# Computing the u side of the 48 first keys densely, beside the v side, in a layer with a product-key expert step

## What is computed

```python
def peer_ffn(h, w_query, sub_keys, expert_u, expert_v):      # 8 heads, 128 x 128 experts of 2048 channels
    q = (h @ w_query).reshape(B, S, PEER_HEADS, 2, PEER_HALF)
    scores = jnp.einsum('bshcd,hckd->bshck', q, sub_keys)
    s_top, i_top = lax.top_k(scores, PEER_TOPK)               # 16 first keys, 16 second keys
    cand_idx = i_top[..., 0, :, None] * PEER_KEYS + i_top[..., 1, None, :]
    best, pos = lax.top_k(cand, PEER_TOPK)                    # 16 experts for each token and head
    gate = jax.nn.softmax(best, axis=-1)
    ...
    u = jnp.take(expert_u, ic, axis=0)                        # 128 rows of 8 KB for each token
    act = jax.nn.gelu(jnp.einsum('ckd,cd->ck', u, xc), approximate=False)
    vv = jnp.take(expert_v, ic, axis=0)
    return jnp.einsum('ck,ckd->cd', gc * act, vv)
```

## Time and profile before

| | us |
|---|---|
| median of 3 runs | 2037.04 (2035.09 to 2037.86) |
| the profiled execution | 2035.97 |
| its span in the trace | 2034.4 |
| end of the query matmuls, groups 0 and 1 under way | 845 |
| end of group 1 on DVE | 882.4 |
| end of group 7 / 12 / 13 / 15 on DVE | 1184.0 / 1482.2 / 1541.8 / 1645.4 |

### The profile page before, as it was taken

One profiled execution on the slowest core, in us unless ns is written; L12 is line 12 of the kernel. 1 busy time (PEld: TensorE's weight loads), 2 busy tenths in 40 slices (PEclk: granted clock), 3 DMA queues, 4 the chain that ended last, 5 costly groups with the idle time before them and its releaser, 6 DMA issues.

```text
span 2034.4 us, 18656 instructions
## 1 busy us (share of the span) xinstructions
PE 1557.4 (77%) x6346; PEld 995.1 (49%) x6347; DVE 1368.9 (67%) x2217; ACT 540.0 (27%) x919; POOL 1050.3 (52%) x647
## 2 busy tenths in 40 slices
PE   7999999999999999622222245656555899999986
PEld 6888888888888898400000011222113554444432
DVE  5463453233333348499889998788889976887977
ACT  5344453345443510110001012232214630000001
POOL 4443343444432413266556675566556737887752
PEclk9999999999999999855555555555555579999998
DMA  8986455665546689599999999999999999999997
GB/s 209 242 176 140 148 186 158 191 189 187 173 133 210 194 298 379 198 409 420 419 416 415 410 417 419 419 418 418 420 418 419 419 357 376 413 415 392 395 422 309
DMA packets 158409, 648.33 MB, mean 319 GB/s; under 512 B 26150, under 2 KB 31342, under 8 KB 96366
## 3 DMA queue, kind: packets, MB, share of 16 engines
q0 software_dynamic: 73728, 450.98, 54.2%
q1 hardware_dynamic: 83824, 195.16, 30.6%
q10 hardware_dynamic: 768, 1.05, 0.2%
HBM read 729.91 MB, written 2.10 MB: 360 GB/s over the span
## 4 chain that ended last, share of the span: by engine, by line
PE 42%; DMA 21%; DVE 15%; issue 11%; POOL 9%; ACTq 0%; ACT 0%; SPq 0%; DVEq 0%; POOLq 0%
PE acc L1673 10%; PE acc L1675 10%; PE acc L1674 10%; DMA u_ring<-in_peer_u_dram,idx 6%; PE acc L2002 4%; DMA v_low<-in_peer_v_dram,idx 4%; DMA u_mid<-in_peer_u_dram,idx 4%; DMA v_more<-in_peer_v_dram,idx 3%; DVE u_ring L1497 3%; DVE u_ring L1495 3%; DVE y_sum L1543 2%; POOL u_ring L628 2%; DMA u_high<-in_peer_u_dram,idx 2%; PE acc L1963 1%; POOL v_high L636 1%
## 5 line engine op out<-in xcount | busy, mean ns | idle before, releaser
L577 POOL TENSOR_TENSOR w_lo<-raw,w_hi 128x1024 fp32r<-128x1024 f32 x112 | 274.7, 2453 | 424.7 <-ACT w_hi L716 424.3
L1673 PE MATMUL acc<-w_hi,t_hi 128*128 128x512 f32 x896 | 355.0, 396 | 0.0
L1675 PE MATMUL acc<-w_hi,t_lo 128*128 128x512 f32 x896 | 349.5, 390 | 0.0
L1674 PE MATMUL acc<-w_lo,t_hi 128*128 128x512 f32 x896 | 349.0, 390 | 0.0
L628 POOL DMA_INDIRECT u_ring<-in_peer_u_dram,idx x160 | 211.6, 1323 | 251.3 <-DVE dots L1497 212.2
L1076 DVE TENSOR_TENSOR w_lo<-raw,w_hi 128x1024 fp32r<-128x1024 f32 x112 | 153.0, 1366 | 265.4 <-ACT w_hi L716 265.3
L716 ACT ACTIVATE w_hi<-raw 128x1024 fp32r<-128x1024 f32 x224 | 237.0, 1060 | 330.5 <-PE acc L1675 287.3
L1495 DVE CUSTOM_DVE_ANT_0 u_ring<-u_ring,hn 128x1024 f32<-128x1024 f32 x160 | 195.6, 1223 | 56.2 <-DMA u_ring<-in_peer_u_dram,idx 50.1
L2041 PE MATMUL misc<-v_low,blocks 128*32 128x512 f32 x368 | 88.5, 1060 | 177.7 <-DMA v_low<-in_peer_v_dram,rows_at 160.6
L2041 PE MATMUL misc<-v_high,blocks 128*32 128x512 f32 x368 | 85.0, 1017 | 157.7 <-DMA v_high<-in_peer_v_dram,rows_at 157.7
L1497 DVE CUSTOM_DVE_ANT_0 u_ring<-u_ring,hn 128x1024 f32<-128x1024 f32 x160 | 195.3, 1221 | 0.0
(11 more groups left out here) (302 smaller groups left out, 2313.7 us busy)
## 6 DMA issues: line engine op xcount, KB each, us to landing
u_ring<-in_peer_v_dram SPq DMA_DIRECT2D x48, 1024.0 KB, 8.8
raw<-in_w_in_dram SPq DMA_DIRECT2D x64, 512.0 KB, 6.5
raw<-in_xattn_wk_dram SPq DMA_DIRECT2D x32, 512.0 KB, 4.5
raw<-in_xattn_wv_dram SPq DMA_DIRECT2D x32, 512.0 KB, 3.9
raw<-in_w_out_dram SPq DMA_DIRECT2D x32, 512.0 KB, 4.7
...
```

The costliest lines, as they stand in the source:

```text
L577: nc.gpsimd.tensor_tensor(w_lo[:, j % RING, :, :], raw[:, j % RING, :, :], w_hi[:, j % RING, :, :].bitcast(F32), ALU.subtract).then_inc(lo ...
L1673: nc.tensor.matmul(o, xh, w_hi[:, s, kk, :], start=first, stop=False)
L1674: nc.tensor.matmul(o, xh, w_lo[:, s, kk, :], start=False, stop=False)
L1675: ins = nc.tensor.matmul(o, xl, w_hi[:, s, kk, :], start=False, stop=last)
```

## The change

For the same 48 first keys the u side is computed densely too.

- SP loads 48 whole tiles of u (128 experts of one first key, 1 MB) into two slots. PE turns a tile in 4 **steps** of 4 transposes (`turn_tile`), ACT copies each quarter out of PSUM (`copy_turned`), and PE multiplies it with the turned hidden rows of all 256 tokens (`tile_dots`, 4 matmuls with 256 columns in a step). ACT takes the gelu of the whole tile into the tables `wT0` and `wT1` (`act_tile`). The 192 steps lie between the picks of groups 2 to 12 on PE and ACT, about 17.5 in a group. The hidden rows are scaled once: DVE widens the factor, PE turns it, ACT copies it, and POOL multiplies `t2f` in 4 instructions in group 2.
- `gather_u` and all v gathers leave out the rows of the 48 keys. The v groups 14 and 15 of the high half are bounded too (`WHOLE` is gone). A u row that is not loaded leaves old data in its slot; its activation is set to zero in `weights`.
- What is scattered is the gate alone, and DVE multiplies it into the tables (`apply_acts`, which takes the place of ACT's copy L943): one instruction of 384 elements in a batch for the low half, three of 128 for the high half. The 16 low batches are all in group 13 (`UNTIL`), one for each k; the 16 high ones in the second half of group 14 and the first half of group 15.
- The half dots write to four bf16 scratch rows and not over the row, and each waits for the half dot that wrote the same scratch before it.
- Slots: u has 5 from group 2 on (was 7); low v has 2 in groups 2 to 7, 3 in groups 8 to 12, 4 after (was 4 to 7). Low v gathers begin in group 2 and are 6 in a group up to group 7, 11 in groups 8 to 12, 12 or 13 after.
- `take_experts(0)` moves from group 1 to group 2, after pick 1; `weights` of the group before moves from pick 2 to pick 9. The order of the first slots of the late stage changes.

```diff
@@ SP
+            for t in range(DENSE):
+                if t < 2:
+                    sp.wait_ge(peer_used, PC)
+                else:
+                    sp.wait_ge(uT_done, 4 * (t - 1))
+                sp.dma_start(u_tile[:, t % 2, :], u_rows[(FROM + t) * KEYS:(FROM + t + 1) * KEYS, :]).then_inc(tile_landed[t % 2], 16)
@@ POOL
                 nc.gpsimd.indirect_dma_start(
                     out=u_slot(n), out_offset=None, in_=u_rows,
-                    in_offset=bass.IndirectOffsetOnAxis(ap=idx[:, p, k:k + 1], axis=0)).then_inc(u_landed[u_index(n)], 16)
+                    in_offset=bass.IndirectOffsetOnAxis(ap=idx[:, p, k:k + 1], axis=0),
+                    bounds_check=FROM * KEYS - 1, oob_is_err=False).then_inc(u_landed[u_index(n)], 16)
...
+                    if p == 2 and k < 8 and k % 2:
...
+                        nc.gpsimd.tensor_tensor(quarter, quarter, rstd_rows[:, :].unsqueeze(1).to_broadcast([P, 4, S]), ALU.mult).then_inc(h_scaled, 1)
@@ ACT
+            def copy_turned(s):
+                act.wait_ge(uT_done, s + 1)
+                if s >= 2:
+                    act.wait_ge(u_products, s - 1)
+                nc.scalar.activation(uT[:, s % 2, :, :], acc[:, 0, 0, :].rearrange("p (a b) -> p a b", a=4), ACT.Copy).then_inc(uT_copied, 1)
+            def act_tile(t):
+                act.wait_ge(u_products, 4 * (t + 1))
...
+                nc.scalar.activation(wT0[:, t, :], acc[:, 1, t % 2, 0:P], ACT.Gelu)
+                nc.scalar.activation(wT1[t // PIECE][:, t % PIECE, :], acc[:, 1, t % 2, P:S], ACT.Gelu).then_inc(acted, 1)
@@ DVE
+            def apply_acts(b):
+                dve.wait_ge(wT_done, b + 1)
+                dve.wait_ge(acted, DENSE)
...
+                    nc.vector.tensor_tensor(wT0[:, :, t:t + WB], wT0[:, :, t:t + WB], made, ALU.mult).then_inc(wT_copied, 1)
...
                 for k in range(TOP):
                     for b in scatters(g, k):
                         one_hots(b)
+                        if b % BATCHES:
+                            apply_acts(b - 1)
@@ PE
+            def turn_tile(s):
...
+                if s:
+                    pe.wait_ge(uT_copied, s)
+                for a in range(4):
+                    ins = nc.tensor.transpose(acc[:, 0, 0, a * P:(a + 1) * P], u_tile[:, t % 2, (4 * i + a) * P:(4 * i + a + 1) * P], ident[:, :])
+                ins.then_inc(uT_done, 1)
+            def tile_dots(s):
+                pe.wait_ge(uT_copied, s + 1)
...
+                for a in range(4):
+                    ins = nc.tensor.matmul(acc[:, 1, t % 2, 0:S], uT[:, s % 2, a, :], t2f[:, 4 * i + a, :],
+                                           start=i == 0 and a == 0, stop=i == 3 and a == 3)
+                ins.then_inc(u_products, 1)
...
+                    for s in u_steps(p, k):
+                        if s == 0:
+                            turn_tile(0)
+                        if s + 1 < STEPS:
+                            turn_tile(s + 1)
+                        tile_dots(s)
                     for n in share[taken(p, k):taken(p, k + 1)]:
                         if n < TILE0 - 1:
                             take_values(n)
+                    for b in scatters(p, k):
+                        scatter_weights(b)
```

More of the change, by code:

```diff
@@ L452, in hybrid_layer @@
         for m in range(len(AT_FIRST), TILE0):
-            free = [s for s in range(V2S) if m < NARROW or s not in (7, 8, 9)]
+            free = [s for s in range(V2S) if m < NARROW or s not in (8, 9)]
             LATE_SLOTS.append(min(free, key=lambda s: max((i for i in range(m) if LATE_SLOTS[i] == s), default=-1)))
@@ L1374, in _ @@
             reciprocal_root(4, 3 * 4 * TT)
+            for t in range(TT):
+                ins = nc.vector.tensor_copy(pick[:, t, :], rstd[:, t:t + 1].to_broadcast([P, P]))
+            ins.then_inc(rstd_wide, 1)
             dve.wait_ge(head_done, 1)
@@ L1519, in period @@
                         route_experts(g + 1)
[L1520 to L1523 removed]
+                    if k == 9:
+                        weights(g - 1)
                     for i in range(1, PH):
@@ L2007, in query_item @@
                         p_scores(i)
+            pe.wait_ge(rstd_wide, 1)
+            for t in range(TT):
+                ins = nc.tensor.transpose(misc[:, 2, S + t * P:S + (t + 1) * P], pick[:, t, :], ident[:, :])
+            ins.then_inc(rstd_turned, 1)
             query_item(1, 0)
@@ L2023, in turn_experts @@
-                nc.tensor.matmul(acc[:, 1, 0, 3 * P:3 * P + TOP], pick[:, 0, :], eighth[:, :], start=True, stop=True).then_inc(experts_turned, 1)
+                bank_read()
+                turned["experts"] += 1
+                nc.tensor.matmul(acc[:, 0, 1, 0:TOP], pick[:, 0, :], eighth[:, :], start=True, stop=True).then_inc(experts_turned, 1)
             def turn_weights(g):
                 pe.wait_ge(weights_picked, g + 1)
-                if g:
-                    pe.wait_ge(blocks_ready, g)
```

314 lines of the change are left out of this document (177 added, 137 removed).

## The result

The changed kernel takes 2100.23 us (median of 4 runs, 2093.77 to 2101.77) against 2037.14 for the kernel before: 1.0305 times as long (95% interval 1.0282 to 1.0329). The forecast was 2029, the range 1992 to 2076. It is slower, and outside the range. The profiled execution, the fastest of the four (2093.77 us), has a span of 2092.1 us, 57.7 more than before; by the medians it is 63.1 more.

What follows compares the result with a forecast made beforehand. The prediction took the DMA engines to set the pace from group 2 to 15, DVE close behind. Terms -11 + 5 - 6 - 23 + 26.4 + 23.4 - 22 = -7 took 2036 to 2029 us, range 1992 to 2076.

Steps and rivals of the forecast that it cites:

- Groups 3 to 12: Groups 3 to 7 at 49.5 us each, -6 in all; groups 8 to 12 at 55 each, -23 in all.
- skipped rows at no cost: In the gather queue, rows left out by the bound take no time; the volume of loaded rows explains the time.
- Rival B: Groups 2 to 12: PE's single line becomes the bound; 1.0 us wait per v row gives 2059 us; chance 0.28.
- Rival D: Groups 2 to 12: the steps run at PE's lower clock, some 400 us more, about 2430; chance 0.03.
- the wait that was set at zero below 9 us: Groups 2 to 12: PE stops, including `bank_read` at pick 10, reach DVE only beyond its 9 us of lead.
- Group 2: About 48 us becomes 53 through POOL's wait for `take_experts(0)` and four multiplications: +5, bounds 0 to +15.
- Groups 13 to 15: The moved batches at PE's lower clock: group 13 +26 to 86 us, groups 14 and 15 +23 to 127.
- Both engines say the same: Group 13: PE's cycles give 86 us and DVE's need gives 83.
- C: Faster rival: PE's clock stays high through group 13, batches halve, 195 us instead of 213 there, 2010; chance 0.20.
- Late stage: Adds finish earlier until PE's end is next late: -20, and 2 more from the tail, -22 (bounds -12 and -29).
- The adds can start and end earlier: Late stage: gathers of groups 14 and 15 shrink by 12.3 MB, so DVE's adds move up to 29 us earlier.
- Group 1: DVE's wait in `take_experts(0)` moves to group 2, so 5 picks come first: -11 us, bounds 0 to -27.

Runs made afterwards that it cites:

- e10: e1 with every gather of groups 2 to 15 taking short rows from all 128 experts, none skipped, same bytes on average: 2055.3 us.
- e1: The changed kernel with its 48 tile loads, but PE takes the steps of only the first two tiles: 2095.9 us.
- e15: e1 with 48 u rows skipped by a fixed pattern: partitions 32 to 63 and 96 to 127 not multiples of 4: 2074.8 us.
- e3: The changed kernel with nearly all u and v rows of groups 2 to 15 left out by the bound, tiles and steps kept: 2027.3 us.
- e2: The changed kernel with all 192 steps, but only the first two tiles loaded and read again: 2046.2 us.
- e9: The changed kernel with 4 more matmuls of 128 columns behind each of the 16 low batches in group 13: 2092.9 us.
- e5: The kernel before with `take_experts(0)` after pick 7 of group 1, not pick 2, and POOL's first two v gathers later: 2026.5 us.

## Why the prediction was wrong

**Groups 3 to 12, the step that failed.** "Groups 3 to 7: 19.2 MB, 46.3 us at 415. Groups 8 to 12: 22.5 MB, 53.8 us at 419." The volumes were right; e10 moves them in 254.5 and 270.5 us, 50.9 and 54.1 a group. The rates were not. They were taken from stretches where most gathers are whole, and there unevenness counts little: u is 16 of 28 gathers and even. With every gather bounded the fullest of 16 engines decides, and the rate is 353 to 374 GB/s (e1). The prediction tested "skipped rows at no cost" only where few rows are skipped. That was the check to distrust: the change moves the share of skipped rows in u from none to 37%, outside what the trace of before could show. Without PE's steps it is worth 5 us a group in groups 8 to 12 and 3 in groups 3 to 7 (e1 against e10), 40 us, as much as the gap there. Making the u skips even gives back 3.0 and 1.1 of that (e15); that the rest is the v skips is not shown.

**Rival B** gave 60 us a group in groups 8 to 12 and was near the time, with the row that it named at 0.54 us as its point of decision. It was wrong: e1 takes PE's work away and nothing moves. That its 60 us lie beside the measured 59.2 is luck: they wanted 1.0 us of wait for a v row, and 0.54 were measured. PE's need was mis-sized by little (50.8, forecast 49.1), and a step was right. On PE's timeline in group 9:

```profile
1297.21 1.89 PE L2139 MATMUL acc<-t2f,uT 128*128 128x256 f32 x8
1298.94 0.60 PE L2127 MATMUL acc<-ident,u_tile 128*128 128x128 f32 x4
1299.38 1.89 PE L2139 MATMUL acc<-t2f,uT 128*128 128x256 f32 x8
```

From one to the next it is 2.17 us, forecast 2.2. **Rival D** fell: the steps hold the clock at 0.95 to 0.97. The Trainium skill's rule that transposes don't count as PE being busy the same way (TensorE: Matmul & The Clock Gate, Part 4: PE-mode transpose) may be so, but a fifth of a step's time in transposes didn't bring the clock down here.

**Group 6**, the wait that was set at zero below 9 us. It took 58.0 us, and PE's and DVE's waits in it are

```profile
PE acc L2116 <- issue: 9.9, 1, 9.9
DVE exp_rec L1499 <- ACT exps L945: 5.4, 1, 5.4
DVE scrap_a L1561 <- DMA u_ring<-in_peer_u_dram,idx: 4.9, 2, 3.5
```

PE waits 9.9 us before a table is turned (`bank_read`, until DVE's pick 10). It reaches DVE in two ways. ACT stands 13.1 us for that table, which it copies before it comes to the exponentials that DVE waits for. And PE's v rows stand behind the table: they end at 1129.81 and 1138.28, POOL's next v gathers go out only at 1130.63 and 1139.11, and the u gathers behind these are late. The lead of the u slots doesn't cover it. Without the steps (e1, e10, e15) the exponentials cost 0.4 us, but PE stands 17.6 to 18.7 us for the table, one u row then comes 6 to 7 us late, and group 6 takes 58.5, 55.6 and 57.4. In e3, without any rows, it still takes 52.9 where its neighbours take 47.8 and 48.4. The step was named, and its price missed by 5 us once.

**Group 2** was named rightly and mis-sized: +14.4 for +5, inside its bounds of 0 to 15. The 7.06 us behind `take_experts(0)` and the slower half dots (2.3 us) were both there; the sum gave them 5 together. DVE waits 12.0 us for u rows in all. In e2, which loads no tile in group 2 where the changed kernel loads four, it waits 6.7, and the group is 5 us shorter: the tiles' loads are a term that the sum didn't have. The Trainium skill (SBUF — State Buffer, Who interferes with whom) says that DVE and GpSimd share a port pair under an exclusive lock; the three lengthened instructions of DVE agree with it. They cost 4.2 us, 1.9 of them still in group 1, and not the 9.8 that the prediction worked out by the rule.

**Groups 13 to 15** came as told on PE: +32.1 and +22.2 for +26.4 and +23.4, at a clock of 0.55, with 5.45 us from one v row to the next and a batch between them:

```profile
1509.60 1.94 PE L2151 MATMUL misc<-v_turned,blocks 128*32 128x512 f32 x8
1511.47 3.65 PE L2184 MATMUL acc<-hotB,hotA 128*128 128x48 f32 x16
1515.05 1.94 PE L2151 MATMUL misc<-v_more,blocks 128*32 128x512 f32 x8
```

"Both engines say the same" failed for DVE: the 57.6 in its need of 83 stands in no row (rows 2 have it busy for 52.77), and it was busy for 75.5 of the 91.7 us, PE for 83.0. The 24 and 20 us around the batches of groups 14 and 15 stand in no row either. C didn't come: the clock fell with the batches, as the earlier trace rows had it, and rose only with more work on PE (e9).

**Late stage.** "The adds can start and end earlier" failed: the bytes saved in groups 14 and 15 only left the DMA engines at 262 GB/s there, while the batches went through PE, and brought nothing forward: DVE's first add starts 3.7 us after group 15's end, where it was 1.2. POOL waits for `got` after group 15 as it did before (28.0, before 25.5 us), and the v gather that hangs on it goes out 43.8 us after group 15's end (1758.73), where it was 37.3. The last low tile and the first sums, the rows that answer:

```profile
2041.27 3.70 PE L2191 MATMUL misc<-u_ring,wT 128*128 128x512 f32 x8 [1.89 <-DMA u_ring<-in_peer_v_dram]
```

```profile
2059.22 2.48 DVE L1645 TENSOR_TENSOR y_sum<-misc,got 128x512 f32<-128x512 f32 x4
```

They are 14.2 us apart, not at once: the adds still come last. The stage is 11.8 us shorter, just below the bound of 12.

**Group 1** was right: -10.1 for -11, and e5 shows the term alone (-11.5). The 1.9 us of the first multiplication, which the prediction had in group 2, lie in it too.
